# S5 state inputs and attention products in strips of 32 columns, alternating scores, a re-laid S5 input, and three moves in a two-layer hybrid decoder

## What is computed

```python
def hybrid_layer(x, ...):
    h = rms_norm(x, norm_g)
    proj = jnp.einsum('bsd,de->bse', h, w_in)
    u_lru, u_s5, qkv_ret, q_nsa, kv_nsa, bg_nsa, gate_paths, merge = split_columns(proj, IN_SIZES)
    y_lru = rg_lru_mixer(u_lru, ...)
    y_s5 = s5_mixer(u_s5, ...)
    y_ret = retention_mixer(...)
    y_nsa = nsa_mixer(...)
    ys = jnp.stack([y_lru, y_s5, y_ret, y_nsa], axis=2) * silu(gate_paths)
    branch = jnp.einsum('bsnw,nwd->bsnd', ys, w_branch)
    merged = jnp.sum(sigmoid(merge) * branch, axis=2)
    return x + jnp.einsum('bsd,de->bse', merged, w_out)
```

## Time and profile before

| | us |
|---|---|
| median of 3 runs | 801.07 |
| lowest and highest run | 799.58, 805.43 |
| profiled execution | 799.71 |
| its span | 797.9 |
| TensorE busy | 776.7 |
| VectorE, ScalarE, GpSimd busy | 477.3, 409.5, 302.8 |

### The profile page before, as it was taken

How to read it: one execution, slowest core, us unless ns; L and a number is a source line. 1 busy time by engine, 2 the same in 40 slices (tenths; PEclk the granted TensorE clock), 3 DMA queues, 4 the chain that set the end, 5 groups by cost and what they waited for, 6 DMA issues and landing times.

```text
span 797.9 us, 12551 instructions
## 1 busy us (share of the span) xinstructions
PE 776.7 (97%) x5022; PEld 659.9 (83%) x5022; DVE 477.3 (60%) x765; ACT 409.5 (51%) x657; POOL 302.8 (38%) x135
## 2 busy tenths in 40 slices
PE   8999899999999999999999998999999999999996
PEld 7888689889888888888888777888898788888885
DVE  2899856583676533524585979276564946154344
ACT  5675424547554654454438644254476435655441
POOL 3000000015777865588100000000555968655750
PEclk9999999999999999999999999999999999999999
DMA  8668454564344644544626955275534445444541
GB/s 243 168 182 267 123 197 132 170 227 132 120 144 133 185 136 131 159 158 162 151 64 171 284 159 177 90 232 189 176 110 139 132 140 181 150 114 155 171 146 53
DMA packets 87001, 126.72 MB, mean 159 GB/s; under 512 B 22072, under 2 KB 32672, under 8 KB 86944
## 3 DMA queue, kind: packets, MB, share of 16 engines
q1 hardware_dynamic: 86768, 125.89, 51.8%
q10 hardware_dynamic: 176, 0.04, 0.0%
HBM read 124.86 MB, written 1.05 MB: 158 GB/s over the span
## 4 chain that ended last, share of the span: by engine, by line
PE 86%; issue 7%; POOL 4%; ACT 1%; DMA 1%; DVE 0%; POOLq 0%; SPq 0%; DVEq 0%; ACTq 0%
PE proj L1656 59%; PE proj L1695 7%; POOL w_lo L679 4%; PE M L1651 4%; PE M L1821 2%; PE proj L1699 2%; PE M L1790 2%; PE M L1986 1%; PE M L1991 1%; PE M L1832 1%; PE M L562 1%; PE M L2010 1%; PE M L2009 1%; PE M L1893 1%; PE M L2008 1%
## 5 line engine op out<-in xcount | busy, mean ns | idle before, releaser
L679 POOL TENSOR_TENSOR w_lo<-raw,w_hi 128x1024 fp32r<-128x1024 f32 x112 | 286.4, 2591 | 447.0 <-ACT w_hi L701 416.8
L701 ACT ACTIVATE w_hi<-raw 128x1024 fp32r<-128x1024 f32 x192 | 198.2, 1054 | 108.6 <-PE proj L1656 69.9
L1656 PE MATMUL proj<-w_hi,h_hi 128*128 128x512 f32 x544 | 216.9, 399 | 4.7 <-issue 3.2
L1656 PE MATMUL proj<-w_hi,h_lo 128*128 128x512 f32 x544 | 212.6, 391 | 0.0
L1656 PE MATMUL proj<-w_lo,h_hi 128*128 128x512 f32 x544 | 212.6, 391 | 0.0
L1656 PEld LDWEIGHTS proj<-w_hi,h_hi 128*128 128x128 f32 x544 | 102.5, 188 | 27.0 <-issue 6.0
L1656 PEld LDWEIGHTS proj<-w_hi,h_lo 128*128 128x128 f32 x544 | 102.5, 188 | 21.9
L1656 PEld LDWEIGHTS proj<-w_lo,h_hi 128*128 128x128 f32 x544 | 102.7, 189 | 20.6 <-issue 0.5
L1241 DVE TENSOR_TENSOR w_lo<-raw,w_hi 128x1024 fp32r<-128x1024 f32 x80 | 94.7, 1220 | 30.1 <-ACT w_hi L701 29.8
L1695 PE MATMUL proj<-h_full,raw 128*128 128x256 f32 x256 | 56.2, 379 | 0.0
L1695 PEld LDWEIGHTS proj<-h_full,raw 128*128 128x128 f32 x256 | 48.3, 190 | 6.5
(11 more groups left out here) (331 smaller groups left out, 1194.4 us busy)
## 6 DMA issues: line engine op xcount, KB each, us to landing
raw<-in_w_in SPq DMA_DIRECT2D x152, 512.0 KB, 4.3
raw<-in_w_branch SPq DMA_DIRECT2D x32, 512.0 KB, 3.7
raw<-in_w_out SPq DMA_DIRECT2D x16, 512.0 KB, 3.6
raw<-in_s_w_glu SPq DMA_DIRECT2D x8, 512.0 KB, 4.6
raw<-in_w_in SPq DMA_DIRECT2D x8, 256.0 KB, 2.6
merged<-in_nsa_ck_w SPq DMA_DIRECT2D x4, 512.0 KB, 6.8
mt<-in_nsa_ck_w SPq DMA_DIRECT2D x4, 512.0 KB, 8.8
merged<-in_nsa_cv_w SPq DMA_DIRECT2D x4, 512.0 KB, 4.7
```

The lines of the kernel that those rows point to most:

```text
L679: nc.gpsimd.tensor_tensor(w_lo[:, slot(s, l), 0:n * w], raw[:, u % N_RAW, 0:n * w], w_hi[:, slot(s, l), 0:n * w].bitcast(f32), ALU.subtrac ...
L701: i = nc.scalar.activation(out_, in_, func, **kw)
L1656: last = mm(dst, left[i], right[j], start=start and n == 0, stop=stop and n == 2, skip_group_check=True)
```

## The change

- `state_inputs`: each matmul becomes four, with 32 columns of the stationary each, to the partitions j to j + 31 of the same place.
- `attention_product`: the same for each of its three products.
- `attention_scores` and `compressed_scores`: the matmuls of the two halves alternate; `compressed_scores` is one call with one signal (`cs_done` is 1 a layer).
- `u_s5` is stored with the four steps of a block outermost, `(j c)`; `own_outputs` reads it so, in contiguous column blocks.
- The transposes of cmp go ahead of the second half of chunk u_lru; ACT's copies of them go ahead of the casts of ret_v.
- `v_sum[1]` moves from `kd` to a free part of `s5x` and to `qT[:, 2:4]`, where cmp_tm lay: DVE waits for `cmpT_done` before its last sum. ACT's nsa_kv copies go ahead of `spread_v(1)` and `keep_y(0)`, and the wait for `vk_ready` is gone.
- On TensorE the first half of gate_s5 goes ahead of `chunk_kernels(1)`.

```diff
@@ -283,8 +283,7 @@
-        kd_flat = kd[:, :, :, :, :, :].rearrange("p a y h u d -> p (a y h u d)")
-        v_sum = [[mt_flat[:, 0:512], mt_flat[:, 1024:1536]], [kd_flat[:, 0:512], kd_flat[:, 512:1024]]]
+        v_sum = [[mt_flat[:, 0:512], mt_flat[:, 1024:1536]], [s5x[:, 2560:3072], qT[:, 2:4, :].rearrange("p a b -> p (a b)")]]
@@ -830,7 +829,8 @@
-                    run(flat(u_s5[:, :, :]), pr("u_s5")[:, :], ACT.Copy, evac("u_s5"))
+                    run(u_s5[:, :, :].rearrange("p q (j c) -> p q j c", j=LC),
+                        pr("u_s5")[:, :].rearrange("p (q c j) -> p q j c", q=KB, j=LC), ACT.Copy, evac("u_s5"))
@@ -841,18 +841,18 @@
                     keep_wT(0, 0)
                     keep_wT(0, 1)
+                    act.wait_ge(cmpT_done, 1)
+                    for h in range(NKV):
+                        for s in range(2):
+                            run(x2[64 * s:64 * s + 64, :, h, :],
+                                pr("cmp")[64 * h:64 * h + 64, 0:512].rearrange("p (m t s) -> p m t s", m=2, s=2)[:, :, :, s],
+                                ACT.Copy, evac("cmp") if h and s else None)
                     cast_units(UNIT_END[CHUNK["u_lru"]] + 1)
                     spread_v(0)
                     cast_units(UNIT_END[CHUNK["u_lru"]] + 2)
                     act.wait_ge(chunk_done, ch("u_lru"))
                     run(u_lru[:, :, 3:T + 3], pr("u_lru")[:, :].rearrange("p (t n) -> p t n", t=KB), ACT.Copy, evac("u_lru"))
                     cast_units(UNIT_END[CHUNK["ret_v"]])
-                    act.wait_ge(cmpT_done, 1)
-                    for h in range(NKV):
...
                     spread_w(1)
@@ -862,9 +862,6 @@
                     trig(1)
-                    spread_v(1)
-                    keep_y(0)
-                    act.wait_ge(vk_ready, 2)
                     act.wait_ge(chunk_done, ch("nsa_kv"))
...
                             evac("nsa_kv") if t else None)
+                    spread_v(1)
+                    keep_y(0)
@@ -1156,6 +1155,8 @@
                         v.tensor_tensor(v_sum[h][0], t[:, 0], t[:, 1], ALU.add)
+                        if h:
+                            dve.wait_ge(cmpT_done, 1)
                         v.tensor_tensor(v_sum[h][1], t[:, 3], t[:, 2], ALU.subtract).then_inc(v_ready, 1)
@@ -1787,7 +1788,9 @@
-                                last = mm(M[:, 2 + f, s * NC5:(s + 1) * NC5], wT[:, f, s, :], uc[:, HS * h + s, :], start=True, stop=True)
+                                for j in range(0, P, 32):
+                                    last = mm(M[j:j + 32, 2 + f, s * NC5:(s + 1) * NC5], wT[:, f, s, j:j + 32], uc[:, HS * h + s, :],
+                                              start=True, stop=True)
@@ -1817,7 +1820,7 @@
-                                    u = u_s5[32 * d:32 * d + 32, 2 * h + q, :].rearrange("p (c j) -> p j c", j=LC)
+                                    u = u_s5[32 * d:32 * d + 32, 2 * h + q, :].rearrange("p (j c) -> p j c", j=LC)
@@ -1840,14 +1843,14 @@
                     turn_w(0, 1)
-                    chunk("u_lru", 1)
-                    state_inputs(0)
                     pe.wait_ge(cmp_read, 2)
...
                     last.then_inc(cmpT_done, 1)
+                    chunk("u_lru", 1)
+                    state_inputs(0)
                     chunk_kernels(0)
@@ -1859,8 +1862,8 @@
                     compress(0, "ck")
+                    chunk("gate_s5", 0)
                     chunk_kernels(1)
-                    chunk("gate_s5", 0)
                     hidden_T(0, "ck")
@@ -1947,21 +1950,21 @@
-                    def compressed_scores(e):
+                    def compressed_scores():
...
-                                last = mm(M[:, e, at:at + 16], nqT[r, h, t * P:(t + 1) * P], kcT[r, (h // 2) * 16:(h // 2) * 16 + 16],
-                                          start=True, stop=True)
+                                for e in range(2):
+                                    r = slice(64 * e, 64 * e + 64)
+                                    last = mm(M[:, e, at:at + 16], nqT[r, h, t * P:(t + 1) * P], kcT[r, (h // 2) * 16:(h // 2) * 16 + 16],
+                                              start=True, stop=True)
@@ -1978,21 +1981,26 @@
+                        early(0, 0)
+                        late(1, 0)
+                        early(0, 1).then_inc(at_even, 1)
+                        late(1, 1)
+                        late(0, 0)
+                        pe.wait_ge(at_even, i + 1)
+                        early(1, 0)
+                        late(0, 1)
+                        early(1, 1).then_inc(at_s, 1)
@@ -2005,9 +2013,11 @@
                         for b, g in enumerate((0, 2, 1, 3)):
-                            mm(M[:, 3, g * HD:(g + 1) * HD], probT[:, 8 + b, :], nv[:, 0, i, :], start=True, stop=True)
-                            mm(M[:, 3, 256 + g * HD:256 + (g + 1) * HD], probT[:, 2 * b, :], nv[:, 0, i, :], start=True, stop=False)
-                            last = mm(M[:, 3, 256 + g * HD:256 + (g + 1) * HD], probT[:, 2 * b + 1, :], nv[:, 1, i, :], start=False, stop=True)
+                            for at, block, key, first, final in ((0, 8 + b, 0, True, True), (256, 2 * b, 0, True, False),
+                                                                 (256, 2 * b + 1, 1, False, True)):
+                                for j in range(0, P, 32):
+                                    last = mm(M[j:j + 32, 3, at + g * HD:at + (g + 1) * HD], probT[:, block, j:j + 32], nv[:, key, i, :],
+                                              start=first, stop=final)
                         last.then_inc(at_o, 1)
```

More of the change, by code:

```diff
@@ L104 @@
     "c_loaded": 64, "chunk_done": 35, "cmpT_done": 1, "cmp_read": 2, "co_done": 1, "cpT_done": 1, "cpT_ready": 1,
-    "cp_ready": 1, "cs_done": 2, "cs_exp": 1, "cs_sub": 1, "cw1_loaded": 128, "cw_done": 1, "cw_loaded": 32,
+    "cp_ready": 1, "cs_done": 1, "cs_exp": 1, "cs_sub": 1, "cw1_loaded": 128, "cw_done": 1, "cw_loaded": 32,
     "dec_ready": 2, "diag_done": 2, "dt_exp": 1, "dt_rows": 1, "evacuated0": 16, "evacuated1": 16, "gate_tanh": 2,
@@ L849, in _ @@
                     cast_units(UNIT_END[CHUNK["ret_v"]])
-                    act.wait_ge(cmpT_done, 1)
-                    for h in range(NKV):
-                        for s in range(2):
-                            run(x2[64 * s:64 * s + 64, :, h, :],
-                                pr("cmp")[64 * h:64 * h + 64, 0:512].rearrange("p (m t s) -> p m t s", m=2, s=2)[:, :, :, s],
-                                ACT.Copy, evac("cmp") if h and s else None)
                     spread_w(1)
@@ L1509, in _ @@
                     gated("ret", ro)
-                    dve.wait_ge(cs_done, 2)
+                    dve.wait_ge(cs_done, 1)
                     shape = [P, TT, 4, 16]
@@ L1948, in _ @@
                     tr(M[:, 1, 0:32], kc[:, :, :].rearrange("p u d -> p (u d)"), 32).then_inc(kcT_done, 1)
-                    def compressed_scores(e):
-                        r = slice(64 * e, 64 * e + 64)
+                    def compressed_scores():
                         for t in range(TT):
@@ L1962, in _ @@
                     pe.wait_ge(kcT_ready, 1)
-                    compressed_scores(0)
-                    compressed_scores(1)
+                    compressed_scores()
                     chunk("merge_lru_1", range(1, 2))
@@ L1980, in attention_scores, with early, late @@
                             pe.wait_ge(at_pT_ready, i)
-                        for e in range(2):
+                        def early(e, n):
+                            r, at = slice(64 * e, 64 * e + 64), (2 * e + n) * P
+                            return mm(M[:, 2, at:at + P], nqT[r, 2 * h + n, 0:P], nkT[r, i, 0:P], start=True, stop=True)
+                        def late(e, n):
                             r = slice(64 * e, 64 * e + 64)
-                            def small_():
-                                for n in range(2):
-                                    at = (2 * e + n) * P
-                                    last_ = mm(M[:, 2, at:at + P], nqT[r, 2 * h + n, 0:P], nkT[r, i, 0:P], start=True, stop=True)
-                                return last_
-                            if e == 0:
-                                small_().then_inc(at_even, 1)
-                            for n in range(2):
-                                mm(M[:, e, n * T:(n + 1) * T], nqT[r, 2 * h + n, P:T], nkT[r, i, :], start=True, stop=True)
-                            if e == 1:
-                                pe.wait_ge(at_even, i + 1)
-                                last = small_()
-                        last.then_inc(at_s, 1)
+                            return mm(M[:, e, n * T:(n + 1) * T], nqT[r, 2 * h + n, P:T], nkT[r, i, :], start=True, stop=True)
+                        early(0, 0)
[7 more added lines that the diff above has]
+                        early(1, 1).then_inc(at_s, 1)
                     def attention_T(i):
```

## The result

The changed kernel takes **764.6 us** (762.85 to 766.98) against 801.0 us of the kernel before on the same chip. The ratio is 0.9538, 95% interval 0.9493 to 0.9584: 36.4 us between the medians, and 4.6% by the ratio. The forecast was 759.7 with a range of 752 to 773. So it is 4.9 us short, and inside the range. The profiled execution took 762.85 us (before: 799.71), which is 36.9 us where the sum said 41.4. How the parts of the sum came out is the subject of what follows; two of them did not come out as written, and one cost was not in the sum at all.

What follows compares the result with a forecast made beforehand. TensorE, busy 97% of the span, was taken as the bound. Terms of 6.6 + 9.7 + 4.4 + 2.7 + 9.2 + 8.3 - 1.2 + 1.7 = 41.4 us gave 758.3, or 759.7 us against the median; range 752 to 773.

Steps and rivals of the forecast that it cites:

- The prices by neighbours: TensorE's new blocks priced from similar matmuls in the old trace, such as 14.1 ns a strip pass from state_outputs.
- Idle of the moves: TensorE's waits before ret_v, chunk_kernels(1) and gate_s5 vanish through the reordering: 8.3 us saved.
- What comes back, -1.2: At nsa_kv, TensorE arrives earlier and waits for DVE's w_lo, 0.5 to 0.6 us a layer: 1.2 us lost.
- The clock, 1.7: In layer 1's gate_s5, the half-clock stretch goes with the idle time ahead of it: 1.7 us saved.
- so many passes by 14.1 ns: State inputs and attention products in strips: pass count times 14.1 ns, plus edges; 6.6 and 9.7 us saved.
- Rival 4: Supply: w_lo, casts or transfers give way as TensorE runs ahead; 5 us lost, 765 us; chance 0.07.
- The stored input: S5's own_outputs reads u contiguously instead of with a 16-byte step: 2.31 us a call, 9.2 us saved.
- The lower end of the range: Whole kernel at 752 us, with scores and compressed scores at their best bounds and both clock falls gone.
- Scores at 0.8 a call: Best bound for alternating halves in attention scores, eight calls; the term itself was 0.55 a call, 4.4 us.
- the second clock fall: Layer 1's slow-clock stretch right after the compressed scores, costing about 1.7 us; the forecast said it may stay.
- Rival 1: S5 outputs stay slow because four strips write one PSUM bank: 9.2 us come back, 769 us; chance 0.14.
- Rivals 2 and 3: State-input and attention-product strips gain nothing (776 us, chance 0.04), or run one after another, slower (811 us, chance 0.02).

Runs made afterwards that it cites:

- run 10: The kernel before with the three moves alone, and the places of v's sums they need: 792.5 us, ratio 0.9907.
- run 2: The changed kernel with the attention products as whole matmuls again: 775.8 us, ratio 0.9677.
- run 4: The changed kernel with u_s5 stored as before and read with the step of four elements: 771.2 us, ratio 0.962.
- run 5: The kernel before with only S5's input stored as it is streamed and read contiguously: 800.0 us, ratio 0.9971.
- run 3: The changed kernel with scores and compressed scores one half after the other again: 772.7 us, ratio 0.9633.

## Why the prediction was right, and where it was not

**The prices by neighbours held.** 14.1 ns a pass for the strips and 0.15 us for the edges (1.96 us a call of the state inputs, 1.92 measured; 1.51 a call of the products, 1.48 measured), 2.34 us for the S5 outputs (2.31), 1.9 for the compressed scores (1.89), 1.76 us an iteration for products and scores together (1.73). The Trainium skill (TensorEngine Tiling (Array Packing), Instruction Overhead) gives each matmul about 60 cycles of overhead. As a price of every instruction in turn, an estimate of 25 ns at 2.4 GHz, it did not show: the passes of L1792 follow each other every 15 ns (1.92 us for 128).

**Idle of the moves**: 8.3 of 8.3, shown alone by run 10. All three waits went.

**What comes back, -1.2, was wrong.** No wait for DVE's w_lo appeared in the changed kernel. TensorE did come to nsa_kv earlier, but the DVE work moved ahead too: the pair of pieces that began at 72.99 begins at 71.53, and the w_lo pieces were ready 0.4 to 2.5 us ahead of their use in the trace. Only run 2, with the products whole, had one, of 1.3 us.

**The clock, 1.7, was under-sized.** Two stretches went, worth 3.0. The sum kept the second, "right after the compressed scores with their 16 columns", without asking what alternating does to it. With alternating halves that block is 1.89 us instead of 3.25, and in the profiled executions the clock never fell there in 20 places.

**What failed is the step "so many passes by 14.1 ns" as a complete price.** It weighed an overhead for each instruction, and found none. It did not ask how fast instructions reach TensorE, since the trace of before showed no wait of that kind. There, state inputs, own outputs, state outputs and `compress` used up 512 instructions in 11.9 us, one block after the other; in the changed kernel they use up 704, in 7.9 us without the waits. Rival 4 named a supply that gives way as TensorE runs ahead, at 5 us, but looked for it in w_lo, casts and transfers, and argued from the shares of DVE, ACT and POOL. The supply that gave way was that of the instructions: 7.0 us. The two errors told just now, 1.2 and 1.3, went the other way and hid a third of it. So the kernel is faster for the reasons given and by nearly the sizes given, but that the time came within 5 us of the forecast is in part luck.

**Nor do the parts add up.** The stored input was priced at 9.2. It was worth 6.6 within the change, and alone 2.3 by the ratio, with 4.5 as the interval's far end, since a faster block runs into the next limit: the instructions, the pause behind it, the clock.

**The lower end of the range does not follow from its terms.** Scores at 0.8 a call give 2.0 us more, compressed scores at 3.2 give 0.5, and the second clock fall 1.7: 759.7 - 4.2 = 755.5, not 752. The result lies above both.

**Rivals.** Rival 1 (S5 outputs stay slow) is refuted by the 380 ns and run 4: bank and row groups are the same with and without the step. The Trainium skill (TensorEngine Tiling (Array Packing), Gotcha 1: PSUM Pressure) says that different row tiles cannot access one bank simultaneously. The trace does not agree: 64 passes with a mean of 214 to 380 ns, from four row groups into one bank, are through in 2.31 us, and the four of a group start within some 20 ns. So in this case the sharing cost nothing that shows. Rivals 2 and 3 (strips gain nothing, or run one after another) are refuted by 8.0 us for 512 passes. Rival 4 came true near its size (5 us priced, 7.0 measured), by another mechanism.

**What stays open.** That a block of instructions is asked for too late, rather than transferred too slowly, is not shown: each of the four waits has its packet close ahead of it, and a packet takes 1 us of the 2.4. What sets a packet's start isn't shown either; in the changed kernel it lies between 5 us before and 4 us after TensorE comes to the packet ahead of it. Why the clock fell in one layer and not in its twin, with the same list (96 in run 5, full speed at the same place in the kernel before), isn't explained either; what the traces show is that every stretch at 1.2 GHz but those at the start and the end stands behind or in a pause, a wait on issue in the middle of a block (2.07 us in run 3, 2.80 in run 2, 2.66 in run 4, 2.20 in run 5), or the compressed scores one half after the other, and that a wait of 2.05 us in the changed kernel had none behind it.

## What to carry to other kernels

Before a wide matmul is split into strips, count the instructions that the whole stretch around it will use up, not only the price of a strip: here stretches that used up a packet's 254 (a load with every matmul) in 2.3 to 3.6 us had waits in the middle of straight code, though not all of them, and in the changed kernel these ate a gain of 6.4 us. Take the fewest strips that bring the gain (two did what four did), and put wide matmuls between blocks of short ones. And measure a part within the whole as well as alone: the same edit was worth nothing or 5 us, and another 2 or 7, by what stood around it.

## What the runs showed of the hardware that I had not expected

- **Two strips are nearly as fast as four.** For 128 rows by 128 columns, 64 moving columns, fp32: whole 14.7 us for 128 passes, two strips 8.3 for 256, four strips 8.0 for 512. That is 115, 65 and 63 ns for a whole tile's worth. Four strips at once do not bring four times.
- **TensorE's instructions come in packets of 16 KB**, about 254 of them, 1 us each, and in all runs TensorE goes on 1.0 to 1.6 us behind a packet's end (1.3 to 1.5 in the changed kernel). A wait of this kind has no semaphore, stands at a packet's boundary by count, mostly in the middle of a block, and cost 0.3 to 0.6 us beyond its own length in the changed kernel, since the passes around it are slower than usual.
- **A step of 16 bytes in the moving fp32 operand costs about 1 ns a column**: 622 against 380 ns for 256 columns, 289 against 214 for 64.
- **A low-use block can cost more behind it than in it**: the compressed scores, at 3.25 us, were followed by a fall of the clock worth 1.6 us in 6 of 8 places of the profiled executions, and at 1.89 us in none of 20.
